# Low parts of 18 down-projection units by accumulating transfers in place of VectorE subtractions

## What is computed

```python
def swiglu(x, w_gate, w_up, w_down):
    return (jax.nn.silu(x @ w_gate) * (x @ w_up)) @ w_down
# 256 x 1024 in, inner width D_FF = 2816 = 22 blocks of 128
```

## Time and profile before

| | us |
|---|---|
| median of 3 runs | 688.74 (688.55 to 688.88) |
| profiled execution | 689.18 |
| its span in the trace | 687.4 |
| TensorE busy | 679.5 (99%) |
| TensorE weight loads busy | 583.7 (85%) |
| VectorE busy | 482.8 (70%) |
| ScalarE busy | 416.7 (61%) |
| GpSimd busy | 89.3 (13%) |
| moved by DMA | 126.13 MB, mean 183 GB/s |

### The profile page before, as it was taken

How to read it: one execution, slowest core, us unless ns; L and a number is a source line. 1 busy time by engine, 2 the same in 40 slices (tenths; PEclk the granted TensorE clock), 3 DMA queues, 4 the chain that set the end, 5 groups by cost and what they waited for, 6 DMA issues and landing times.

```text
span 687.4 us, 9325 instructions
## 1 busy us (share of the span) xinstructions
PE 679.5 (99%) x3736; PEld 583.7 (85%) x3736; DVE 482.8 (70%) x730; ACT 416.7 (61%) x706; POOL 89.3 (13%) x173
## 2 busy tenths in 40 slices
PE   9999999999999999999999999999999999999996
PEld 7888888888888888888888988888888888888885
DVE  6878796767666666666455767777868877777774
ACT  7787775765555555555655866665577755555553
POOL 3122020788200000010810000000000000000001
PEclk9999999999999999999999999999999999999999
DMA  9935534736555555537343336555453655555401
GB/s 338 397 127 225 204 122 153 282 126 244 184 188 187 196 198 199 195 126 272 127 155 148 125 122 219 194 193 179 157 213 131 230 198 184 184 189 189 174 1 61
DMA packets 19484, 126.13 MB, mean 183 GB/s; under 512 B 2416, under 2 KB 2544, under 8 KB 5232
## 3 DMA queue, kind: packets, MB, share of 16 engines
q1 hardware_dynamic: 19296, 125.34, 50.3%
q10 hardware_dynamic: 144, 0.20, 0.1%
HBM read 124.48 MB, written 1.05 MB: 183 GB/s over the span
## 4 chain that ended last, share of the span: by engine, by line
PE 95%; DVE 2%; ACT 1%; DMA 1%; issue 0%; SPq 0%; POOLq 0%; POOL 0%; ACTq 0%
PE bank L434 92%; PE bank L442 3%; DMA first<-in_first_dram 1%; DVE wlo L1442 0%; ACT whi L1000 0%; DVE yy L1450 0%; DVE xa L1442 0%; ACT uT L997 0%; DVE xres L1442 0%; ACT L997 0%; DVE yy L1442 0%; SPq L394 0%; POOLq L2124 0%; DVE last L1442 0%; DVE uT L1442 0%
## 5 line engine op out<-in xcount | busy, mean ns | idle before, releaser
L1442 DVE TENSOR_TENSOR wlo<-raw,whi 128x1024 fp32r<-128x1024 f32 x222 | 270.6, 1231 | 61.1 <-ACT whi L1000 57.6
L1000 ACT ACTIVATE whi<-raw 128x1024 fp32r<-128x1024 f32 x222 | 230.1, 1052 | 5.6 <-PE bank L434 4.7
L434 PE MATMUL bank<-xb,whi 128*128 128x512 f32 x496 | 124.2, 392 | 0.5 <-DVE sg L1442 0.5
L434 PE MATMUL bank<-xa,whi 128*128 128x512 f32 x432 | 108.3, 392 | 0.0
L434 PEld LDWEIGHTS bank<-xb,whi 128*128 128x128 f32 x496 | 90.4, 188 | 17.8 <-DVE sg L1442 0.7
L434 PE MATMUL bank<-whi,xb 128*128 128x512 f32 (+1 forms) x320 | 94.6, 373 | 0.0
L434 PEld LDWEIGHTS bank<-xa,whi 128*128 128x128 f32 x432 | 78.9, 188 | 15.5
L434 PEld LDWEIGHTS bank<-xb,wlo 128*128 128x128 f32 x496 | 67.7, 190 | 4.9
L434 PE MATMUL bank<-whi,hh 128*128 128x512 f32 (+1 forms) x180 | 69.7, 387 | 0.0
L434 PE MATMUL bank<-wlo,hh 128*128 128x512 f32 (+1 forms) x180 | 69.6, 387 | 0.0
L434 PE MATMUL bank<-whi,hl 128*128 128x512 f32 (+1 forms) x180 | 69.2, 384 | 0.0
(11 more groups left out here) (246 smaller groups left out, 791.3 us busy)
## 6 DMA issues: line engine op xcount, KB each, us to landing
raw<-in_w_dram SPq DMA_DIRECT2D x109, 1024.0 KB, 4.8
first<-in_first_dram SPq DMA_DIRECT2D x8, 388.0 KB, 6.7
raw<-in_w_dram SPq DMA_DIRECT2D x4, 512.0 KB, 9.1
bias<-in_bias_dram SPq DMA_DIRECT2D x1, 1024.0 KB, 7.9
xres<-in_x_dram SPq DMA_DIRECT2D x1, 1024.0 KB, 8.3
gain<-in_ffn_norm_w_dram SPq DMA_DIRECT2D x1, 512.0 KB, 9.1
gain<-in_mix_norm_g_dram SPq DMA_DIRECT2D x1, 512.0 KB, 9.8
gain<-in_ffn_norm_g_dram SPq DMA_DIRECT2D x1, 512.0 KB, 5.1
```

The source lines that it names most:

```text
L434: return e.matmul(o, l, r, start=start, stop=stop)
L1000: return e.activation(o, i, ACT.Copy, **options)
L1442: return e.tensor_tensor(out=o, in0=a, in1=b, op=op)
```

## The change

For the down units of blocks 0 to 17 of the first gated layer (`ADDED`: unit to block number) ScalarE writes, right behind the high part, its negative into `wlo`. GpSimd, behind the angles, issues for each of the 18 units one transfer from `raw` into `wlo` with addition, 128x1024, SBUF to SBUF. VectorE leaves these units out. TensorE and SyncE wait for the transfer (three semaphores in turn) where they waited for VectorE.

```diff
+ADDED = {u: f for what, f, u in ffn_plan(FFN_1) if what == "dn" and f < NF - HOLD}
...
+    s_add = [semaphore(f"add{i}") for i in range(3)]
...
+    def added(u):
+        return s_add[ADDED[u] % 3], 16 * (ADDED[u] // 3 + 1)
...
@@ sync: load(c)
             if c >= NR + 2:
-                w.wait_ge(*dve.of("lo", 2 * (c - NR) + 1))
+                for u in (2 * (c - NR), 2 * (c - NR) + 1):
+                    w.wait_ge(*(added(u) if u in ADDED else dve.of("lo", u)))
...
@@ tensor: ffn
                 if what == "dn" and f < NF - HOLD:
-                    w.wait_ge(*dve.of("lo", u))
+                    w.wait_ge(*(added(u) if u in ADDED else dve.of("lo", u)))
...
@@ scalar: hi_to
                 copy(whi[u % NH][:, :], raw_of(u)).then_inc(*act.done("hi", u))
+                if u in ADDED:
+                    w.wait_ge(*act.now())
+                    copy(wlo[u % NH][:, :], whi[u % NH][:, :].bitcast(F32), scale=-1.0).then_inc(*act.done("negated", u))
...
@@ vector: lo_to
-                w.wait_ge(*act.of("hi", u))
-                low(wlo[u % NH][:, :], raw_of(u), whi[u % NH][:, :]).then_inc(*dve.done("lo", u))
+                if u not in ADDED:
+                    w.wait_ge(*act.of("hi", u))
+                    low(wlo[u % NH][:, :], raw_of(u), whi[u % NH][:, :]).then_inc(*dve.done("lo", u))
...
@@ gpsimd: between the angles and root(2, 0)
         ts(c_, c_, TWO_PI / 4, None, ALU.add).then_inc(*pool.done("angles"))
 
+        for u in ADDED:
+            w.wait_ge(*act.of("negated", u))
+            e.dma_start(wlo[u % NH][:, :], raw_of(u), accum_op=ALU.add).then_inc(*added(u)[:1], 16)
+
         root(2, 0)
```

## The result

| | before | after |
|---|---|---|
| median of the runs, us | 688.64 (4 runs) | 718.6 (718.28 to 719.35, 4 runs) |
| ratio | | 1.0432 (95%: 1.042 to 1.0445) |
| profiled execution, span | 689.18, 687.4 | 718.43, 716.7 |

A forecast was written before the change was run, and what follows sets the result against it. The prediction took TensorE, busy 99%, as the bound. A stall of 165 + 5.5 - 142.4 = 28.1 us plus a restart of 2 gave +30 us, a median of 718.8, rounded to 719; range 711 to 742.

The forecast's parts named there:

- What bounds the kernel: Whole kernel and this stage: TensorE, busy 99% of the span; relieving VectorE, busy 70%, cannot shorten it.
- Where GpSimd is: At unit 40, due about 142.4 us: GpSimd begins the angles only at 146.03, so its transfers behind them stall TensorE.
- The chain's end: GpSimd's angle steps, faster beside an idle VectorE, end at 165 us instead of 176.80; bounds 164 and 176.8.
- three missing subtractions: VectorE's removed subtractions for units 40, 43 and 46 no longer stretch GpSimd's steps: 2.5 us in all.
- The transfer: Unit 40's accumulating 512 KB transfer: 5.5 us from GpSimd's issue to landing, bounds 3.5 and 9.8.
- The restart: TensorE after the stall runs at half pace for about 4 us: 2 us lost, bounds 0 and 4.
- The sum: At the first down unit: stall 28.1 us plus restart 2, +30 us on the profiled 689.18.
- What was costed at nothing: Later 15 transfers, ScalarE's negations, SyncE's loads, DMA engine time, VectorE's removed subtractions and work behind the stall: no cost or saving.
- The cover: Units 49 to 91, judged by unit 55: 12.6 us from negation to TensorE's use, against 5.5 for a transfer.
- B: Rival: GpSimd's angle chain gets no faster and ends at 176.8, giving 731 us; 12%.
- C: Rival: accumulating transfers over 12.6 us each, or 4.0 of engine time, stop TensorE at later down units; 726 to 748; 12%.
- D: Rival: not slower, GpSimd reaches its transfer loop by 136.9, before unit 40 is due; 688.7 us; 2%.

The follow-up runs named there:

- Experiment 6: Changed kernel without the 18 transfers (low parts wrong, only negated high parts; TensorE and SyncE wait for ScalarE's negation); 688.91 us, ratio 0.9999 to the kernel before.
- experiment 3: Changed kernel, all 18 transfers, with the whole angle chain moved earlier in GpSimd's program, ahead of the chunked attention's roots; 697.37 us, ratio 1.0123.
- experiment 2: Changed kernel with only the down units from 52 on (14 of 18) on the new path, the earlier ones with VectorE; 694.61 us, ratio 1.0081.
- experiment 1: Changed kernel with only the down units from 58 on (12 of 18) on the new path, the earlier ones with VectorE; 688.96 us, ratio 0.9998.
- experiment 8: Changed kernel plus 18 VectorE subtractions of 128x1024 from two SBUF tiles into a scratch tile during the stall; 735.22 us, ratio 1.0669.
- experiment 7: Changed kernel plus 112 unused matmuls of 128x512 on TensorE ahead of its wait for unit 40's transfer; 717.33 us, ratio 1.0414.
- experiment 4: Changed kernel with the angle chain moved earlier in GpSimd's program and the first two transfers issued between the masks' steps; 690.78 us, ratio 1.0023.
- experiment 10: Changed kernel with the new path only from unit 58 on, plus 11 GpSimd memsets (about 2.9 us) ahead of each transfer; 689.68 us, ratio 1.0016.
- experiment 9: Changed kernel with the new path only from unit 58 on, plus 25 GpSimd memsets (6.5 us) ahead of each transfer; 699.41 us, ratio 1.0137.
- experiment 5: Changed kernel with the angle chain moved earlier and the new path only from unit 49 on (15 of 18); 689.03 us, ratio 0.9999.

## Why the prediction was right

*What bounds the kernel.* Right. Experiment 6 takes 21.1 us off VectorE, with no transfer to wait for, and gains nothing.

*Where GpSimd is.* Right, and it is the whole case: the place of the loop in GpSimd's program. The loss goes with how late GpSimd is at the first unit of the new path: 27.2, 6.6, 3.4 and 0 us of waiting in the kernel after and experiments 3, 2 and 1.

*The chain's end*, forecast at 165: 164.9. The mechanism is shown by experiment 8. The 2.5 us that I took for three missing subtractions were right in sum; part of them came before 146, since the angles began at 144.2. VectorE fell idle at 150.7 (the low part of the product at 150.23 + 0.43), not at 152.3. That the end fits to 0.1 us is in part luck: with the same GpSimd program ahead of them, the angles began at 144.2 in the kernel after, 145.4 in experiment 7 and 143.4 in experiment 8.

*The transfer*, forecast at 5.5 us (3.5 to 9.8): 4.8 for unit 40, with no load on the engines' queues. This term was 0.7 too high, which is most of the error of the sum.

The Trainium skill's estimate (DMA: Bandwidth & Descriptors, Anatomy of one DMA), quoted in the prediction, was 3.2 us, or 4.4 with the source counted twice; the trace has 4.8 alone and 7.6 beside loads, so the second reading is the closer one and only for an idle machine.

*The restart*, 2 us: 2.1 by unit 40's length, and experiment 7 takes 2.0 of that away.

The sum: 27.2 waited against 28.1, 2.1 against 2.0.

*What was costed at nothing.* The cover held for the 15 later transfers, but by less than I wrote. I gave them 5.5 of their 12.6 us; all 18 took 7.6 in the median and 11.8 at most, beside loads whose own landing went from 4.8 to 6.7 us between 210 and 290 us. GpSimd's issue and TensorE's use of that slowest one, and its landing time:

```profile
225.91 0.86 POOL L2096 DMA_DIRECT2D wlo<-raw  x1 [7.45 <-ACT wlo L1009]
238.23 0.40 PE L443 MATMUL bank<-whi,hh 128*128 128x512 f32 x1
```

```profile
wlo<-raw POOLq DMA_DIRECT2D x1, 512.0 KB, 11.8
```

It was in time by 0.5 us. The engine time was right: 7.0% of 716.7 us for 18 transfers is 2.8 us each (forecast 2.9), against 1.4 for 512 KB of loads (47.6% for 125.34 MB). *"Every later down unit repeats this pattern"* holds in the kernel after (this unit was negated at 225.6, 12.6 us ahead of its use), but not at the layer's beginning: without the stall, unit 46 has 8.8 us and is late (experiment 4), and unit 49, one of the 15, was negated at 156.3 for a use at 167.4, 11.1 us. The working took every unit for unit 55 and every landing for 5.5 us, and the result did not punish it.

*The rivals.* B fell by experiment 8. C did not come, since no transfer took more than 12.6 us and TensorE waited at no later unit, but the slowest was in time by 0.5 us only. With 2.9 us of delay experiment 10 loses 0.7 us, with 6.5 us experiment 9 loses 10.4. D: the kernel is as fast as before only where the early units stay with VectorE (experiment 1 with 12 units on the new path, or experiment 5 with 15 and the angles moved); even then nothing is gained. No version here beats the kernel before.

## What to carry to other kernels

Before work is moved to an idle engine, read that engine's timeline at the moment when the first piece is due, not its share over the span: GpSimd was busy 13%, and 21.6 of the 30.0 us are one chain of small steps that stood in the way (experiment 3); most of the rest is the masks ahead of it. Relief of VectorE, for which TensorE never waited in this stage, had a ceiling of zero, and a run that leaves the work out shows such a ceiling at once. How long a chain of short GpSimd steps takes depended on VectorE's two-input instructions beside it: the last 46 angle steps took 14.1 us beside an idle VectorE and 30.9 in experiment 8. Where work has a cover, compare it with the slowest landing, not the median: 11.8 and 7.6 us here.

## What had not been expected of the hardware

The clock of TensorE fell to its lower level not only after the long stall: it did so after waits of 2.42 and 2.07 us (experiment 9), but not after one of 1.74 us (experiment 4, granted clock 1.00 from 160.85 to 166 in the stretches after it) or 1.15. A restart at 1.2 GHz cost 1.6 to 2.1 us by the length of the unit behind the wait (4.37 and 4.44 us in experiment 9, 4.82 in the kernel after, against 2.75), nearly as much as the short wait itself.

An accumulating transfer of 512 KB within SBUF, issued by GpSimd, takes 0.86 us of GpSimd's time (up to 1.5), landed in 4.4 to 5.0 us in the quickest cases (4.7 with no load in the queues), in 7.6 in the median beside a 1 MB load every 5.5 us, and in 11.8 at most in the kernel after (10.3 for unit 46 of experiment 4, 12.1 for one in experiment 2).
